# Two PSUM banks instead of six in the feed-forward stages, and the S5 set-up in 14 early steps instead of 33

## The reference

```python
# first block, feed-forward, each layer
u = causal_dwconv(h @ w_up[l], ffn_conv_w[l], ffn_conv_b[l])     # 1024 -> 5632, three taps
val, gate = jnp.split(u, 2, axis=-1)
x = x + g2 * ((jax.nn.silu(gate) * val) @ w_down[l])             # 2816 -> 1024
# second block, S5 mixer: what depends on parameters only
step = jnp.exp(log_dt)[:, None]
lam_bar = jnp.exp(lam * step)                                    # complex, 64 states x 32 groups
b_bar = ((lam_bar - 1.0) / lam)[..., None] * (b_re + 1j * b_im)
# second block, feed-forward, each layer
x = x + jnp.square(jax.nn.relu(h2 @ w_ff1[l])) @ w_ff2[l]        # 1024 -> 4096 -> 1024
```

## Time and profile before

| | us |
|---|---|
| median of the runs | 2351.09 |
| the profiled execution | 2351.09 |
| its span | 2349.2 |
| PE busy with matmuls | 2206.8 (94%) |
| PE weight loads | 2097.7 (89%) |
| DVE busy | 1661.5 (71%) |
| ACT busy | 1416.4 (60%) |
| POOL busy | 200.7 (9%) |
| chain that ended last: PE, DVE, ACT | 71%, 14%, 10% |

### The profile page before, as it was taken

The page is one execution under the profiler, slowest core; times in us unless marked ns, Lnnn a source line. Parts: engine busy times, 40 slices in busy tenths (PEclk is TensorE's granted clock), DMA queues, the critical chain, the costliest instruction groups (busy, mean ns, idle before and its releaser), DMA issues.

```text
span 2349.2 us, 42627 instructions
## 1 busy us (share of the span) xinstructions
PE 2206.8 (94%) x17568; PEld 2097.7 (89%) x17568; DVE 1661.5 (71%) x2998; ACT 1416.4 (60%) x2203; POOL 200.7 (9%) x178
## 2 busy tenths in 40 slices
PE   2989999999999899999999899899999989899999
PEld 2979899999999798999999887689999987799999
DVE  5898778578768887686779673646687663646653
ACT  3577887466546788864764556664643548564542
POOL 0000000022000000000322111000030111000000
PEclk9999999999999999999999999999999999999999
DMA  7455556567755555565564422345565323344553
GB/s 282 171 163 181 178 181 221 182 207 231 235 186 169 162 189 169 198 218 169 182 193 156 144 84 89 100 151 164 180 189 185 121 66 108 107 153 144 193 191 128
DMA packets 110593, 394.64 MB, mean 168 GB/s; under 512 B 12320, under 2 KB 13888, under 8 KB 110272
## 3 DMA queue, kind: packets, MB, share of 16 engines
q1 hardware_dynamic: 96768, 343.47, 44.8%
q0 software_dynamic: 11904, 43.03, 5.7%
q10 hardware_dynamic: 1728, 5.43, 0.6%
HBM read 390.83 MB, written 1.05 MB: 167 GB/s over the span
## 4 chain that ended last, share of the span: by engine, by line
PE 71%; DVE 14%; ACT 10%; issue 3%; DMA 1%; POOL 0%; SPq 0%; DVEq 0%; ACTq 0%
PE bank L549 70%; ACT scr L1035 4%; DVE WL L1537 3%; ACT WH L1035 3%; ACT L1024 2%; DVE arena L1601 2%; DMA ring<-in_w 1%; ACT arena L1035 1%; DVE arena L2232 1%; DVE scr L1584 1%; PE bank L629 1%; DVE scr L1790 1%; DVE arena L1715 1%; DVE scr L1777 0%; DVE small L1789 0%
## 5 line engine op out<-in xcount | busy, mean ns | idle before, releaser
L1035 ACT ACTIVATE WH<-ring 128x1024 fp32r<-128x1024 f32 (+1 forms) x638 | 669.9, 1052 | 740.5 <-PE bank L549 716.4
L549 PE MATMUL bank<-HTH,WH 128*128 128x256 f32 x3392 | 977.3, 288 | 15.3 <-DVE HTL L1574 5.1
L549 PE MATMUL bank<-HTL,WH 128*128 128x256 f32 x3392 | 962.2, 284 | 0.0
L549 PE MATMUL bank<-HTH,WL 128*128 128x256 f32 x3392 | 961.4, 283 | 0.0
L1537 DVE TENSOR_TENSOR WL<-ring,WH 128x1024 fp32r<-128x1024 f32 (+2 forms) x602 | 735.1, 1230 | 191.7 <-ACT WH L1035 189.5
L549 PEld LDWEIGHTS bank<-HTH,WH 128*128 128x128 f32 x3392 | 648.9, 191 | 28.3 <-issue 26.3
L549 PEld LDWEIGHTS bank<-HTL,WH 128*128 128x128 f32 x3392 | 649.0, 191 | 3.1 <-issue 2.8
L549 PEld LDWEIGHTS bank<-HTH,WL 128*128 128x128 f32 x3392 | 648.9, 191 | 0.0
L1024 ACT ACT_TABLE_LOAD x120 | 154.0, 1283 | 43.3 <-PE bank L549 25.8
L549 PE MATMUL bank<-ff2h,WH 128*128 128x256 f32 x512 | 144.0, 281 | 0.0
L549 PE MATMUL bank<-ff2l,WH 128*128 128x256 f32 x512 | 143.8, 281 | 0.0
(11 more groups left out here) (318 smaller groups left out, 3743.7 us busy)
## 6 DMA issues: line engine op xcount, KB each, us to landing
ring<-in_w SPq DMA_DIRECT2D x620, 512.0 KB, 4.0
arena<-in_wada POOLq DMA_DIRECT2D x80, 512.0 KB, 4.7
ring<-in_w SPq DMA_DIRECT2D x16, 384.0 KB, 3.2
arena<-in_wada SPq DMA_DIRECT2D x8, 512.0 KB, 19.3
arena<-in_wada ACTq DMA_DIRECT2D x8, 512.0 KB, 22.0
ring<-in_w SPq DMA_DIRECT2D x8, 288.0 KB, 2.8
XT<-in_xt SPq DMA_DIRECT2D x1, 1024.0 KB, 9.2
arena<-in_s POOLq DMA_DIRECT2D x4, 256.0 KB, 4.1
```

The costliest lines, as they stand in the source:

```text
L549: ins = e.matmul(out, a, b, start=(start and i == 0), stop=(stop and i == len(pairs) - 1))
L1035: return e.activation(out, a, func, **kw)
```

## The change

Three things change. First, every group takes bank 0 or 1 in turn, in all stages. Second, `s5set` has 14 steps, 12 of them in the up phase, where it had 33: most `yield`s inside it are gone, so a step issues more at once. Its scratch tiles move to rows 5 and 6 of `scr` (rows 0 and 1 for the two last steps), and with that its wait for the end of the up phase is gone. Third, POOL's `powers` run at units 14, 18 and 22.

```diff
-            first = len(self.groups)
             for g in build(l):
                 g.stage = st
-                banks = (0, 1, 2, 3, 6, 7) if build in (stage_b, stage_d) else (0, 1)
-                g.bank = banks[(len(self.groups) - first) % len(banks)]
+                g.bank = len(self.groups) % 2
...
-S5_TICKS = {stage_b: [5, 10, 15, 20, 24, 28, 32, 36] + turn_ticks(46, 25, 17, 25),
-            stage_d: [3, 6, 10, 14, 18, 22, 26, 30] + turn_ticks(34, 25, 26, 25)}
+S5_TICKS = {stage_b: [4, 6, 8, 11, 14, 17, 20, 23, 26, 29, 33, 37, 50, 56],
+            stage_d: [4, 6, 8, 10, 12, 14, 16, 18, 20, 22, 25, 28, 38, 44]}
...
                 serial(e.tensor_tensor(th, lim, step, ALU.mult), V)
-                yield
                 reduce_angle(th, tm, V, "angle", l)
-                yield
                 yield
...
-                w0, w1, w2, w3 = (scr[:, i // 2, 256 * (i % 2):256 * (i % 2) + 256].rearrange(
+                w0, w1, w2, w3 = (scr[:, 5 + i // 2, 256 * (i % 2):256 * (i % 2) + 256].rearrange(
...
-                p.wait_ge(s5_in(l), ev_vector("fflo", 1, 21) if l == 0 else ev_vector("ff2lo", 0, 15))
+                p.wait_ge(s5_in(l))
...
                     serial(e.tensor_tensor(w3, fr, b, ALU.mult), V)
-                    yield
                     e.tensor_tensor(gr, w0, w1, ALU.add).then_inc(V.inc(), 1)
...
-                    m0, m1 = (scr[:, 2 + i, 0:16 * n].rearrange("p (a b) -> p a b", b=n) for i in range(2))
+                    m0, m1 = (scr[:, (5 if n < 16 else 0) + i, 0:16 * n].rearrange("p (a b) -> p a b", b=n)
+                              for i in range(2))
...
                     if n < 32:
-                        if n < 16:
-                            yield
                         doubled()
-                    yield
+                    if n > 1:
+                        yield
...
-                    late = 46 if l == 0 else 36
-                    if at in (late, late + 6, late + 12):
-                        powers(l, 2 - (at - late) // 6)
+                    if at in (14, 18, 22):
+                        powers(l, {14: 2, 18: 1, 22: 0}[at])
```

More of the change, by code:

```diff
@@ L971, in tensor_program @@
                     "heads0": lambda l: heads(l, 0), "heads1": lambda l: heads(l, 1), "cutm": lambda l: empty(1),
-                    "s5": s5, "s5set": lambda l: empty(33)}
+                    "s5": s5, "s5set": lambda l: empty(14)}
             live = {}
@@ L1384, in s5set @@
                 yield
-                yield
                 p.wait_ge(L.V("half", l))
                 act(cs, tm, ACT.Sin).then_inc(L.A.inc("cos", l), 1)
-                for i in range(29):
+                yield
+                for i in range(11):
                     yield
@@ L2031, in s5set @@
                 e.tensor_scalar(lr, ar_, -1.0, None, ALU.add).then_inc(V.inc(), 1)
-                serial(e.tensor_tensor(r4, r, r, ALU.mult), V)
-                yield
+                e.tensor_tensor(r4, r, r, ALU.mult).then_inc(V.inc(), 1)
                 e.tensor_tensor(u1, re, re, ALU.mult).then_inc(V.inc(), 1)
@@ L2096, in s5set @@
                     e.tensor_tensor(m1, fb, cb, ALU.mult).then_inc(V.inc(), 1)
-                    if n == 32:
-                        yield
                     e.tensor_tensor(ga, fa, cb, ALU.mult).then_inc(V.inc(), 1)
                     serial(e.tensor_tensor(gb, fa, sb_, ALU.mult), V)
-                    if n > 8:
-                        yield
                     e.tensor_tensor(ga, ga, m0, ALU.subtract).then_inc(V.inc(), 1)
```

## The result

The changed kernel took 2376.39 us (2373.18 to 2376.77, 4 runs), the kernel before 2352.59 (2347.50 to 2356.69, 4 runs) beside it: ratio 1.0088, 95% interval 1.0065 to 1.011. It is slower, as predicted, but by about twice the +10.4 of the sum, and it lies above the range (2349 to 2373). The profiled executions, 2371.44 against 2351.09, differ by 20.35.

The account below looks back on a forecast made before the run. PE, busy 94% of the span, was taken to bound the kernel, so DVE, POOL and bank changes count only where PE waits. 1.6 + 11 - 8.2 + 5 + 1 = +10.4 us on 2351.09 gave 2361.5, eight-in-ten range 2349 to 2373.

Parts of the forecast that it names:

- Term 1: Stage B0: two banks alone make an early convolution late for PE, +1.6 us.
- Term 2: B1's up phase: DVE's packed set-up steps and POOL's work make PE wait for banks, +11 us, ends 5 and 15.
- first part: B1's first groups: late first convolution, early steps and ACT's table loads grow the stall from 1.5 to about 4.3 us by unit 12.
- just even: B1's up phase, unit 14 on: DVE's own steps need 13.8 us against 14.6 free, before POOL's work is added.
- 6 + 3: B1's up phase: DVE delays of 6 us from POOL's `powers` and about 3 from its `lo`.
- Five such meetings: B1, units 12 to 30: DVE held behind POOL's `lo` five times, 0 to 2.2 us each, about 3 in all.
- 1.5 of slack: B1's up phase: lateness that a group without a step can still absorb, taken off 8.2 to give 6.7 us.
- Term 3: B1's down phase: most set-up steps leave it, so PE's waits there go, -8.2 us; the gain could be as small as 6.5.
- Term 4: Stage D0, units 8 to 23: set-up steps beside POOL's `powers` make DVE late beyond its slack, +5 us, ends 0 and 8.
- Term 5: B1 and D0: PE's waits may bring one more fall of the granted clock, +1 us, between 0 and 3.5.
- C: B1 and D0: the shared port excludes whole instructions at each meeting, +21 us, 2372 in all; chance 0.18.

Follow-up runs that it names:

- banks alone: The kernel before with two banks in B and D, set-up and POOL as before; ratio 1.0012 to the kernel before.
- powers held: The changed kernel with POOL's `powers` at their old units in B1 and held back in D0 until the up phase's last result; ratio 1.0030 to the kernel before.
- filler run: The changed kernel with 14, 12 and 16 idle matmuls before the first wait of B1's units 14 and 26 and D0's unit 13; ratio 1.0114 to the kernel before.
- six banks: The changed kernel with six banks back in stages B and D; ratio 1.0073 to the kernel before.

## Why the prediction was wrong, by its steps

- **Term 1** (+1.6) was right: 1.4 in the changed kernel and with banks alone.
- **Term 2** (+11) is the step that failed, by the cost that it gave POOL's work; it was 18.2. Its first part held: 4.3 forecast by unit 12, 3.7 measured, and 4.6 in all with POOL's work taken away. The count of DVE's own steps held too: from the convolution at 1143.85 to that at 1203.12 there are eight groups, 31.6 of own work and 14.3 of steps as they take undisturbed, 45.9 in all against PE's 45.4, "just even". The failed part is what POOL costs, forecast as 6 + 3 and then cut to 6.7 by free time and slack. Measured, with both of POOL's jobs against neither: 131.8 - 118.2 = 13.6, of which 9.6 are waits and 4.0 the two falls of the clock behind them. The eight groups took 59.3 us, so 12.0 of delays stood in DVE's queue, where I had 9, and one idle stretch of 1.36, behind the first fall, in which ACT's WH had waited 3.09 for PE. "Five such meetings at 0 to 2.2 each, are about 3" was the worst line: `lo` alone costs 8.0, or 6.4 without its fall of the clock. I read the rows as saying why: a meeting also lengthens POOL's `lo`, holds ACT up behind the product, and so comes back as a late WH. And the 1.5 of slack was taken off although the first groups had used it up.
- **Term 3** (-8.2) was right: -8.5, with the clock's fall of the earlier trace rows in it.
- **Term 4** (+5) was right in mechanism and in its total: 5.4 of waits, all of it POOL's `powers`, as the sum had it (18.7 against 16.5 and 5.0 of slack would have given nothing without them, and with powers held there was nothing). The place was not: the sum ran to unit 23, and the waits stand at units 11 and 13 alone, where the coefficients and C0 lie beside `powers` and before any block of CS. That the totals agree so closely is in part luck.
- **Term 5** (+1, at most 3.5) was too small. Three falls of the clock stand in B1 and D0 (6.8, 3.4 and 3.4 us long), and by PE's lateness they cost 4.0 and 1.6. They came with PE's waits, and those of B1 were gone when POOL's work was. With the two terms taken apart so, Term 2 is short by 3.2 and Term 5 by 4.6. What a kernel without the falls and with the same meetings takes is not measured, since the filler run had other meetings.

Of the rivals, C was nearest (2372). Its Term 2 of 15 fits the 14.2 of waits, its 3 for the clock is less than the 5.6, and its Term 4 of 8 is more than the 5.4. Its reason was that each meeting excludes a whole instruction; the prediction held the row of 1.64 against it, beside "POOL's instructions of 1.2". That was a misreading. The row of 1.20 at 1709.89 in the earlier trace rows holds two instructions, of 0.62 each, and around that of 1.64 the rows of the kernel before are these:

```profile
1713.13 1.64 DVE L1537 TENSOR_TENSOR WL<-ring,WH 128x1024 fp32r<-128x1024 f32 x1
1713.77 1.60 POOL L2307 TENSOR_TENSOR arena<-trig 128x256 f32<-128x256 f32 x1
1714.70 1.23 DVE L1699 TENSOR_TENSOR scr<-scr 128x512 f32<-128x512 f32 x1
1715.33 1.19 POOL L2308 TENSOR_TENSOR arena<-arena 128x256 f32<-128x256 f32 x1
```

They end at 1714.77, 1715.37, 1715.93 and 1716.52: by turns, each 0.6 behind the other engine's. The Trainium skill's rule (SBUF — State Buffer, Who interferes with whom), that the one who starts first holds the port for its whole instruction, agrees with this, and with the rows at 1155.30 and 1180.75. It does not speak against the 0.84 in place of 0.42 at 1187.85 either: there DVE's instructions and POOL's (0.81 in place of 0.62) alternate one by one, some 0.77 from start to start. So the rule was sound, and what failed was the price put on it. What no rival had is that the position of a step within POOL's four-unit period is worth 20 us (137.8 against 117.2, with 8.1 of it the clock's).

Open: I have not separated, within the 8.0 of `lo`, DVE's own wait from the delay that goes round through ACT. Nor did a kernel with POOL's work held back in both stages keep the two banks, so what two banks cost then was not measured. And how much of the 4.0 of the clock in B1 could be had back stays open, for the reason given.

## What to carry to other kernels

When work is packed closer on one of two engines that share a path to memory, price it by a clean and a disturbed row of the same step, not by one instruction: 2.26 became 4.95, and 3.3 became 8.8. Then ask where in the other engine's period the step falls, and when that engine really starts its work, which is not what its place in the program says. And a change of PE's pace, by a fall of the clock or by filler, shifts the engines against each other: before its gain or loss is read from the total, look whether the same meetings are still there.

## What the runs showed of the hardware that was not expected

- Small instructions suffer most beside `powers`. Among DVE's 16-column ones, 0.17 clean, many took 0.5 to 0.7; with 256 columns 0.42 became 0.84 to 0.96, with 1024 1.22 became 1.52 to 1.76. The addition is 0.3 to 0.5 whatever the size, so it goes by the number of instructions.
- The exclusion goes both ways: of the ten `lo` of POOL in the changed kernel's up phase of B1 four took 2.41 or 2.42, and three, where DVE's steps met them, 3.7 to 3.9.
- The granted clock fell at or behind waits of PE of 1.9 to 4.2 us in B1 and D0 of all these kernels, but not at each (there was none at the wait of 3.40 at unit 14 with six banks). With three waits filled it stayed at 1.00 through 132 us.
